# Mixture-of-experts passes of up to 96 rows: gate/up with the weights stationary, down with 32-row groups stationary in four column parts

## The reference, cut to what matters

```python
logits = (h @ w_router + b_router)             # h: (1024, 1024), 32 experts
top_val, top_idx = lax.top_k(logits, 4)
gates = softmax(top_val)
# for each expert e, over the rows routed to it:
gu   = xb @ w_gu[e] + b_gu[e]                  # 1024 -> 2 x 1024
gate = minimum(gu[:, :1024], 7.0)
up   = clip(gu[:, 1024:], -7.0, 7.0)
act  = gate * sigmoid(1.702 * gate) * (up + 1.0)
y    = act @ w_dn[e] + b_dn[e]                 # 1024 -> 1024
```

## Time and profile before

| what | value |
|---|---|
| median of three runs | 2250.13 us |
| the profiled execution | 2249.16 us, its span 2247.6 us |
| PE busy | 2180.5 us, 97% of the span |
| first pass of up to 96 rows starts on PE | 615.87 us |
| the six passes of up to 96 rows | 615.87 to 834.05 us |
| the fifteen passes of 97 to 128 rows | 834 to 1429 us |
| the twelve wider passes | 1429 to about 2116 us |

### The profile page before, as it was taken

One profiled execution on the slowest core, in us unless ns is written; L12 is line 12 of the kernel. 1 busy time (PEld: TensorE's weight loads), 2 busy tenths in 40 slices (PEclk: granted clock), 3 DMA queues, 4 the chain that ended last, 5 costly groups with the idle time before them and its releaser, 6 DMA issues.

```text
span 2247.6 us, 49018 instructions
## 1 busy us (share of the span) xinstructions
PE 2180.5 (97%) x19538; PEld 1638.1 (73%) x19538; DVE 986.1 (44%) x2155; ACT 391.8 (17%) x814; POOL 617.9 (27%) x932
## 2 busy tenths in 40 slices
PE   8999999999699999999999999999999999999998
PEld 5555566544356568787878878899999999999443
DVE  4664467355743434343443434433333322222474
ACT  3110166411311111111101101100000000000344
POOL 0455588100413131212122122122221111111320
PEclk9999999999799999999999999999999999999999
DMA  5100011321499999999999999888888766652550
GB/s 203 43 25 6 25 50 46 164 75 47 164 387 387 385 383 406 351 359 349 357 339 344 335 341 331 321 309 310 305 292 293 271 239 238 221 194 118 196 183 38
DMA packets 102597, 530.03 MB, mean 236 GB/s; under 512 B 22548, under 2 KB 26436, under 8 KB 50412
## 3 DMA queue, kind: packets, MB, share of 16 engines
q1 hardware_dynamic: 76892, 465.58, 56.0%
q0 software_dynamic: 25616, 63.22, 8.2%
HBM read 497.89 MB, written 27.56 MB: 234 GB/s over the span
## 4 chain that ended last, share of the span: by engine, by line
PE 90%; DVE 3%; issue 3%; ACT 2%; POOL 1%; DMA 1%; SPq 0%; POOLq 0%; DVEq 0%; ACTq 0%
PE ps L2001 19%; PE ps L2004 17%; PE ps L2017 10%; PE ps L2027 9%; PE ps L2047 6%; PE ps L1742 5%; PE ps L2074 3%; PE ps L2126 3%; PE ps L1847 2%; PE ps L1731 2%; PE ps L1853 2%; PE ps L1761 1%; PE ps L1795 1%; PE ps L1827 1%; PE ps L1726 1%
## 5 line engine op out<-in xcount | busy, mean ns | idle before, releaser
L2001 PE MATMUL ps<-xT,wg 128*128 128x144 f32 (+5 forms) x3072 | 437.8, 304 | 6.1 <-issue 6.0
L2001 PEld LDWEIGHTS ps<-xT,wg 128*128 128x128 f32 x3072 | 430.9, 190 | 12.0 <-issue 8.9
L2004 PEld LDWEIGHTS ps<-xT,wg 128*64 128x64 f32 x7680 | 383.5, 137 | 11.6 <-issue 11.6
L2004 PE MATMUL ps<-xT,wg 128*64 128x112 f32 (+2 forms) x7680 | 387.0, 263 | 0.4 <-issue 0.4
L1555 DVE TENSOR_SCALAR gb<-ps,bcur 128x256 f32<-128x256 f32 x216 | 104.6, 484 | 582.5 <-PE ps L2004 325.0
L955 ACT ACTIVATE sg<-gb 128x256 f32<-128x256 f32 x216 | 90.0, 417 | 926.6 <-DVE gb L1555 926.6
L2017 PE MATMUL ps<-actT,wd 128*128 128x144 f32 (+5 forms) x1536 | 218.3, 304 | 0.0
L2017 PEld LDWEIGHTS ps<-actT,wd 128*128 128x128 f32 x1536 | 215.3, 190 | 1.6
L2027 PE MATMUL ps<-wd,actT 128*128 128x512 f32 x480 | 210.0, 595 | 0.0
L621 POOL DMA_INDIRECT xg<-normalised_rows,rowc x184 | 178.0, 967 | 74.1 <-issue 45.7
L2027 PEld LDWEIGHTS ps<-wd,actT 128*128 128x128 f32 x480 | 90.0, 190 | 109.9 <-issue 108.8
(11 more groups left out here) (439 smaller groups left out, 2437.4 us busy)
## 6 DMA issues: line engine op xcount, KB each, us to landing
wg<-in_w_gu SPq DMA_DIRECT2D x264, 1024.0 KB, 6.9
wd<-in_w_dn SPq DMA_DIRECT2D x132, 1024.0 KB, 6.4
expert_rows<-yb POOLq DMA_DIRECT2D x60, 128.0 KB, 5.0
expert_rows<-yb POOLq DMA_DIRECT2D x28, 160.0 KB, 6.1
hT<-in_x_cm SPq DMA_DIRECT2D x8, 512.0 KB, 7.4
cumb<-gate_sums SPq DMA_DIRECT2D x4, 1024.0 KB, 4.7
x<-in_x_tm SPq DMA_DIRECT2D x1, 4096.0 KB, 13.4
wout<-in_w_out SPq DMA_DIRECT2D x1, 4096.0 KB, 20.8
```

The lines of the kernel that those rows point to most:

```text
L2001: ins = m.matmul(ps[:, f % 2, g_ * W:g_ * W + w], wg[:, f, k, g_, :], xT[:, k, 0:w], start=(k == 0), stop=(k == KT - 1))
L2004: ins = m.matmul(ps[c:c + 64, f % 2, g_ * W:g_ * W + w], wg[:, f, k, g_, c:c + 64], xT[:, k, 0:w], start=(k == 0), stop=(k == KT - 1))
```

## The change

1. `narrow_pass`, `bias_rows`, `bb`, `actB`, `act_turned`, `y_narrow` and DVE's loop for these passes go. Passes of up to 96 rows run in `expert_pass` and `wide_pass`, as those of 97 to 128 rows do, with the gate/up of L2004 at w = 96, all eight slices f one after another.
2. Their down keeps the 32-row groups in four column parts, but goes f by f: for each f, three groups, four parts. `dn_mm` counts come after every second f.
3. Router: `fold_parts(5)` and `fold_parts(6)` go between the two halves of a projection of tile 7, and DVE's `logits(6)` goes between the attention part and the state-space part of `resid(7, 1)`.
4. Bias rounds: all three go on PE ahead of the row-number matmuls; on ACT, round 0 comes in the middle of the gate columns, round 1 after them, round 2 after `tokens_in(0)`. The ten reads of the loop bounds come on PE ahead of the wait for round 2.

```diff
@@ pool @@
-            pool.wait_ge(S("cnt_mm"), 4)
-            bias_rows(e0)
...
-                if narrow:
-                    bias_rows(e)
@@ act @@
             gates_turned(0)
-            for part in range(4):
-                gates_in(1, part)
-            gates_turned(1)
+            gates_in(1, 0)
             act.wait_ge(S("hs_st"), 16 * 8)
             bias_out(0)
+            for part in range(1, 4):
+                gates_in(1, part)
+            bias_out(1)
+            gates_turned(1)
             tokens_in(0)
-            tokens_in(1)
-            bias_out(1)
-            tokens_in(2)
-            tokens_in(3)
             bias_out(2)
+            for q in range(1, 4):
+                tokens_in(q)
...
-            with act.Fori(0, ends[0]) as b:
-                ...
-            for c, w in list(enumerate(WIDTHS))[1:]:
-                with act.Fori(ends[c - 1], ends[c]) as b:
+            for c, w in enumerate(WIDTHS):
+                with act.Fori(ends[c - 1] if c else 0, ends[c]) as b:
@@ dve @@
-            resid(7, 1)
+            resid_attn(7, 1)
+            logits(6)
+            resid_ssm(7, 1)
             dve.wait_ge(S("wo_evac"), 16)
             v.nop().then_inc(S("x1_ready"), 1)
-            logits(6)
             logit_parts(7)
...
-            with dve.Fori(0, ends0) as b:
-                ...
-            with dve.Fori(ends0, end) as b:
+            with dve.Fori(0, end) as b:
                 wide_pass(b)
@@ pe @@
-            attn_part(7, 1)
+            attn_part(7, 1, range(0, 2))
             fold_parts(5)
+            attn_part(7, 1, range(2, 4))
             route(6)
-            ssm_part(7, 1)
+            ssm_part(7, 1, range(0, 2))
+            fold_parts(6)
+            ssm_part(7, 1, range(2, 4))
             turn_block(7, 0)
-            fold_parts(6)
             turn_block(7, 1)
...
             bias(0, (2, 3, 4, 5), False)
-            gates_turn(1)
             pe.wait_ge(S("wo_evac"), 20)
             rows_in(1)
             bias(1, (2, 3, 4, 5), False)
+            gates_turn(1)
+            pe.wait_ge(S("wo_evac"), 24)
+            rows_in(2)
+            pe.wait_ge(S("ht_evac"), 11)
+            bias(2, (2, 3, 4, 5), False)
...
-            pe.wait_ge(S("ht_evac"), 11)
-            pe.wait_ge(S("wo_evac"), 24)
-            rows_in(2)
-            bias(2, (2, 3, 4, 5), False)
-            pe.wait_ge(S("wo_evac"), 28)
             pe.wait_ge(S("tab_ld"), 16)
             ends = [pe.value_load(...) for c in range(NW)]
             npass = ends[NW - 1]
+            pe.wait_ge(S("wo_evac"), 28)
...
+                if w == WIDTHS[0]:
+                    for f in range(FT):
+                        if f % 2 == 0:
+                            pe.wait_ge(S(f"dn_ld{f // 2}"), b * 16 + 16)
+                        pe.wait_ge(S("act_ready"), b * FT + f + 1)
+                        for r in range(NGR):
+                            for j in range(4):
+                                ins = m.matmul(ps[GR * j:GR * j + GR, 2 + r // 2, 256 * (r % 2):256 * (r % 2) + 256], actT[:, f, GR * r:GR * r + GR],
+                                               down_cols(f, j, 1), start=(f == 0 and r % 2 == 0), stop=(f == FT - 1), skip_group_check=True)
+                        if f % 2:
+                            ins.then_inc(S("dn_mm"), 1)
+                    return
```

More of the change, by code:

```diff
@@ L61 @@
 NGR = WIDTHS[0] // GR
-NU = 2 * NGR
 NW = len(WIDTHS)
@@ L927, in _ @@
             ends = [act.value_load(passrow[0:1, 4 * c + 3:4 * c + 4], min_val=c + 1, max_val=MAXPASS) for c in range(NW)]
[L928 to L940, removed]
-            with act.Fori(0, ends[0]) as b:
-                for ut in range(NU):
-                    if ut >= 2:
-                        act_turned(b, ut - 2)
-                    act.wait_ge(S("g_ready"), b * FT + ut + 1)
-                    a.activation(sg[0:64, ut % 2, :], gb[0:64, ut % 2, :], ACT.Sigmoid, scale=1.702).then_inc(S("sig_ready"), 3 if ut == NU - 1 else 1)
-                act_turned(b, NU - 2)
-                act_turned(b, NU - 1)
-                y_narrow(b)
-            for c, w in list(enumerate(WIDTHS))[1:]:
-                with act.Fori(ends[c - 1], ends[c]) as b:
+            for c, w in enumerate(WIDTHS):
+                with act.Fori(ends[c - 1] if c else 0, ends[c]) as b:
                     for f in range(FT):
@@ L956, in _ @@
                     if w <= P:
-                        y_out(b)
+                        y_out(b, D if c else 256 * NGR)
             def ple_norm(t):
@@ L1314, in _, with resid_attn @@
             link(v.reciprocal(rss[:, :], rss[:, :]))
-            def resid(t, n):
+            def resid_attn(t, n):
                 w = 2 * t + n
@@ L1321, in resid, with resid_ssm @@
                 link(v.scalar_tensor_tensor(xx, ps[:, WO_BANK[w], :], rss[:, 8 + t:9 + t], xx, ALU.mult, ALU.add))
+            def resid_ssm(t, n):
+                w = 2 * t + n
+                xx = x1[:, t, n * 512:n * 512 + 512]
                 dve.wait_ge(S("wo_mm"), w + 1)
                 v.scalar_tensor_tensor(xx, ps[:, WO_BANK[w] + 1, :], rss[:, t:t + 1], xx, ALU.mult, ALU.add).then_inc(S("wo_evac"), 1)
+            def resid(t, n):
+                resid_attn(t, n)
+                resid_ssm(t, n)
             def norm_rows(t):
@@ L1840, in row_squares, with attn_part @@
                 ins.then_inc(S("ss_mm"), 1)
-            def attn_part(t, n):
+            def attn_part(t, n, ks=range(4)):
                 w = 2 * t + n
@@ L1845, in attn_part, with ssm_part @@
                     pe.wait_ge(S("wo_evac"), w - 1)
-                for k in range(4):
+                for k in ks:
                     ins = m.matmul(ps[:, WO_BANK[w], :], attnT[:, k, t * P:t * P + P], wout[:, k, n * 512:n * 512 + 512], start=(k == 0), stop=(k == 3))
-                ins.then_inc(S("wa_mm"), 1)
-            def ssm_part(t, n):
+                if ks[-1] == 3:
+                    ins.then_inc(S("wa_mm"), 1)
+            def ssm_part(t, n, ks=range(4)):
                 w = 2 * t + n
-                for k in range(4):
+                for k in ks:
                     ins = m.matmul(ps[:, WO_BANK[w] + 1, :], ssmT[:, k, t * P:t * P + P], wout[:, 4 + k, n * 512:n * 512 + 512],
                                    start=(k == 0), stop=(k == 3))
-                ins.then_inc(S("wo_mm"), 1)
+                if ks[-1] == 3:
+                    ins.then_inc(S("wo_mm"), 1)
             def project(t, n):
```

86 lines of the change are left out of this document (4 added, 82 removed).

## The result

The kernel after takes 2233.9 us (median; 2232.2 to 2235.5) against 2250.0 us of the kernel before beside it: a ratio of 0.993, 95% interval 0.9918 to 0.9943, so 0.7% faster, 16.1 us. The forecast was 2232.5 us. Its profiled execution has a span of 2231.0 us, where before had 2247.6.

What follows compares the result with a forecast made beforehand. The prediction took PE's stream of matmuls, busy 97% of the span, as the bound. Six narrow passes give 10 us and the earlier start 7.5, together 17.5 us off the median of 2250.13: 2232.5 us, range 2216 to 2246.

Steps and rivals of the forecast that it cites:

- The pace of gate/up: Narrow-pass gate/up at 96 rows: 41.66 ns per record, extrapolated from wider passes, 21.26 us for 512 records.
- (b): Rival: weight loads set the floor of gate/up, which stays at 24.7 us, a pass 37.7; total 2253 us; chance 0.08.
- The down: Narrow-pass down: 24 rounds of four parts, 192 records, take 10.6 us including the switch from gate/up.
- The stall: Last third of a narrow pass: PE's instruction supply near the loop's back edge; stays at 2.4 us, bounds 0 and 3.5.
- The first pass: First narrow pass: the 2.5 us it loses to the lower clock stay, on top of 34.3 us.
- The start: PE's start of the first pass moves from 615.87 to 608.0 to 608.4: 7.5 us, bounds 5.5 and 8.2.
- the router: Ahead of the passes: moving logits(6) on DVE shortens the chain by some 0.8 us, bounds 0 and 1.3.
- The tight place: Moved bias rounds must fit into PE's 5.38 us idle time before the row-number matmuls; 1.5 us allowed if late.
- The DMAs: Narrow passes ask for 399 GB/s, above the mean of 387, below slices of 420 to 428; costed at nothing.
- (a): Rival: the stall at the loop's back edge goes, 6 x 2.4 us less, 2218 us; chance 0.12.
- (c): Rival: the start of the first pass doesn't move, as reads or bias rounds hold it; 2240 us; chance 0.11.
- (d): Rival: longer code shifts the stall to uncovered places, 2 to 3 us a pass; 2248 to 2275 us; chance 0.06.

Runs made afterwards that it cites:

- gu64: Kernel after, with narrow-pass gate/up moving 64 rows instead of 96, the other 32 left out; 2206.0 us.
- before_again: Kernel before, unchanged, run again on a chip without the stall; 2226.5 us.
- passes_only: Kernel after with the old router order, bias rounds and place of the reads, so parts 1 and 2 alone; 2214.4 us, ratio 0.9954 to the kernel before.
- after_again: Kernel after, unchanged, run again on a chip without the stall; 2207.7 us, ratio 0.9925 to the kernel before.
- pad64_b: Kernel after with 64 empty PE instructions ahead of the loops, on a chip with the stall; 2239.8 us, kernel before 2252.4 there.
- no_gather_b: Kernel after with POOL's indirect gathers replaced by small plain copies from the third pass on, on a chip with the stall; 2213.7 us, kernel before 2252.4 there.
- late_gather: Kernel after with the gathers issued some 10 us later, behind the writes of the pass's results, on a chip with the stall; 2313.5 us, ratio 1.029.
- pad64: Kernel after with 64 empty PE instructions ahead of the loops, on a chip without the stall; 2209.8 us, ratio 0.9931 to the kernel before.
- bunched: Kernel after with SP reloading wg after four slices and wd after the whole down, on a chip without the stall; 2209.2 us.
- no_gather: Kernel after with POOL's indirect gathers replaced by small plain copies from the third pass on, on a chip without the stall; 2210.0 us.
- head_only: Kernel before with parts 3 and 4 of the change alone; 2222.1 us against 2226.0, ratio 0.9982.

## Why the prediction was right, point by point

**The pace of gate/up.** 41.66 ns per record was extrapolated from three widths; the chain gives 41.54 (21.27 us for 512). The line over the moving rows goes on to 64 rows, 29.5 ns in `gu64`. So (b) was wrong with some room, as the 48.34 ns of the earlier trace rows had said against the figure of the Trainium skill, TensorE: Matmul & The Clock Gate, section LDWEIGHTS.

**The down.** 10.6 us forecast, 10.50 measured. The old pass without its stall was put at 33.6 us and is 33.49 in `before_again`; the new one was put at 31.9 and is 31.77.

**The stall.** Its size was right (2.4 forecast, 2.2 measured), so passes two to six came 34.0 us apart against 34.3. Its cause was wrong. I read it as PE's instruction supply near the back edge of a loop; it comes while POOL works on its indirect gathers, on chips that have it. What I had seen is explained by it: the gathers are issued when xT is turned, at the start of the down, so in the narrow passes the stall falls into its last third; and the long matmuls of the passes of 97 to 128 rows cover it. The guess that cover decides was the useful half. The step that failed is the reading of three places near a loop's end as an effect of the end; I had run nothing that tells the two apart, and POOL's timeline beside PE's would have raised the question: in the second pass of before the gathers run from 682.19 to 687.00, and PE goes on at 687.83.

**The first pass.** Forecast 36.8 us (34.3 and 2.5 for the clock), measured 40.2: the one term that was off, by 3.4 us. Chain of waits of the kernel after, first pass, then POOL's timeline and the DMA view from 606 to 646 us:

```profile
606.51 5.90 PE ps L1954 x71
612.41 1.05 issue
613.46 6.26 PE ps L1954 x145
...
619.85 5.44 PE ps L1954 x127
625.29 0.66 issue
625.95 5.50 PE ps L1954 x127
631.45 0.61 issue
632.06 1.87 PE ps L1954 x40
```

```profile
607.80 1.00 POOL L618 DMA_INDIRECT xg<-normalised_rows,rowc  x1 [1.11 <-issue]
...
611.61 0.95 POOL L618 DMA_INDIRECT xg<-normalised_rows,rowc  x1 [0.30 <-issue]
```

```profile
q8 instruction: 5, 0.08, 0.8%
```

Two things are in it. First, the gathers for the second pass run from 607.80 to 612.56, and PE, idle for 1.05 us, goes on at 613.46, 0.9 us after the fourth, as in the other places. In the kernel before these gathers ended at 615.54, ahead of PE's first matmul at 615.87: they fell beside the reads. Hiding the reads moved PE's start into them. The 71 records up to 613.46 take 6.95 us instead of 2.95, of which 1.05 is this and the rest mostly the lower clock up to 611.9. In `passes_only` and `after_again`, on chips without the stall, no such stop is there; the first passes of `pad64_b`, `no_gather_b` and `late_gather`, on chips with it, have it.

Second, the later stops are 127 records apart, 256 instructions with their loads, and the instruction queue moves one packet for each such block, 6.1 us apart (617.6, 623.5, 629.6, 635.8 and 642.0). The new gate/up uses up 256 instructions in 128 x 41.5 ns = 5.3 us; the old one (8.63 us for 160 records) in 6.9 us, and its first pass has no such stop. `passes_only` (0.61 and 0.65 us), `pad64` (0.75 and 0.61) and `after_again` (0.56 and 0.59) have two each; in `bunched` (1.21 and 0.88), `no_gather` (1.19 and 1.15), `no_gather_b` (1.21 and 0.61) and `pad64_b` (0.66 and 1.71) some are longer. That the loop doesn't fetch again held (no such packet from 646 to 817 us); what I had not asked is what its first iteration costs: 1.3 us. The Trainium skill, Runtime: NRT & Kernel Launch, section Instruction fetch mechanics, has blocks of 256 instructions, and the distance of the stops agrees. No run changed the fetches, but `gu64` changed the pace at which PE uses them up, to 3.9 us a block. Chain of waits in its first pass:

```profile
624.89 2.76 issue
627.65 3.95 PE ps L1955 x127
631.60 2.17 issue
```

The stops stay 127 records apart and grow from 0.6 to 2.2 and 2.8 us, so that PE goes on at 621.00, 627.65 and 633.77, 6.7 and 6.1 us apart, where the kernel after goes on at 619.85, 625.95 and 632.06. This is what a supply of one block in some 6.1 us or more looks like; that the packets are what PE waits for is still read from their times and not from a run that moved them.

**The start.** Forecast 7.5 us (5.5 to 8.2), measured 9.36. The parts, from the traces of before and after: up to the router's last tiles 1.4 us, which the change doesn't touch and which differs by 1 us between two traces of the kernel before (545.38 and 544.33) too; the router 1.1 us (forecast 0.8); from `logits(7)` to the first gather 42.67 to 42.19 us, 0.5 (forecast 0.7); from the gather to PE's first matmul 12.95 to 6.58 us, 6.4 (the reads of the bounds, now hidden). Without the first part it is 7.9 us, and the traces of the section on the result, 608.0 against 615.2 to 616.4, put it at 7.6: the forecast was nearer than the 9.36 of this pair of traces says. `head_only` has the same parts, with 6.8 us from the gather to PE. The tight place, bias rounds ahead of the row numbers, held.

**The DMAs.** Costed at nothing: right. 399 GB/s was the forecast for the passes, 417 measured; the 387 of the earlier trace rows were what the old passes asked for, not what the DMAs could do. Where PE asks for more, as in `gu64`, the rate stays at 417. The gain of the whole change is 16.1 us on the one kind of chip (12.6 in the single `pad64_b`) and 16.2 and 17.6 on the other: without the stall the old passes save 2.5 us and from the fourth on give 0.6 of it back in waits for `wg`, the new ones save 2.2 and give nothing back.

**Rivals.** (a), the stall gone, was right as a state of the chip, not as an effect of the change: 2207.7 us. (c) didn't happen. (d) didn't either, but `late_gather` shows what it would have looked like, with another cause.

**The total.** The sum was 17.5 us and 16.1 came: passes two to six 1.5 us better (9.8 for 8.3), the start 1.9 better, the first pass 3.4 worse, the tail 0.75 worse, and the medians a little apart from the profiled executions. That the total came within 1.4 us is in part luck. The first pass took back what the start and the other five passes had brought beyond the forecast, its stop came from the gathers of which the prediction knew nothing, and the 1.9 us of the start lie within the spread of that start. The stall was carried over at the right size for a wrong reason: had its place in the code been the cause, the same number would have come.

What stays open: by which way the gathers slow PE's supply of instructions (or whatever it is that PE lacks), and what differs between the chips. The runs tell only that they do, and that 64 instructions more ahead of the loop don't move the stall. They don't separate POOL's work on the gathers from the transfers that the gathers cause.

## What to carry to other kernels

Where a stall without a wait on data comes at a fixed place of a loop, lay the other engines' timelines beside it before blaming the code's place, above all POOL's indirect DMAs, and put these beside long matmuls: ten microseconds later, beside short ones, they cost 3.6% here, on a chip with the stall. When a loop's body gets faster, ask of its first iteration whether instructions arrive at the new pace. And a new order ahead of a loop should be counted from one event to the next (projection to logits, logits to gather, gather to the first matmul), and over several traces, since the start itself moves by up to 4.6 us for nothing.

## What the runs showed of the hardware that I had not expected

- Four indirect gathers of POOL (1.0 us each, 5 us together) hold PE to four or five records in 0.73 us until 0.8 to 1.0 us after the last of them. In two groups of runs of four, each on a chip of its own, the same code shows nothing of it. Without the gathers a chip that has the stall gave 2213.7 us against 2239.8 with them (and 64 empty instructions), and one that has none 2210.0 against 2207.7. This is as much as the kernel before differs between the two kinds of chip, 2250 against 2225 us; for that kernel it wasn't tried.
- Behind stops of 0.3 to 0.5 us each the clock was at its lower level for some 3.5 us in some passes of `late_gather` (mean 0.95 over 36.8 us, 1.7 us more) and stayed at the upper one in others.
- Column-tiled float32 matmuls with 64 stationary columns follow the moving rows down to 29.5 ns per record at 64 rows.
- The DMAs of one core sustain 417 to 420 GB/s over 160 to 171 us, with `wg` released slice by slice or four at a time.
- In the first iteration of the narrow loop the instruction queue moves a packet every 6 us or so; code that uses 256 instructions in 6.9 us doesn't stop, in 5.3 us it stops for 0.6 to 1.7 us at each block, in 3.9 us for 2.2 to 2.8.
